# Gate/up products of two pairs of chunks in Strassen form (seven block products for eight), weight sums made by VectorE

## The reference, cut to what matters

```python
def swiglu(h, w_gate, w_up, w_down):
    return (jax.nn.silu(h @ w_gate) * (h @ w_up)) @ w_down
# four times:  x = x + 0.5 * swiglu(rms_norm(x, g), w_gate, w_up, w_down)
# once:        x = x + (silu(gate) * up) @ w_down,  gate, up = split(h @ w_gate_up, 2)
```

## Time and profile before

| | |
|---|---|
| time, median of 3 runs | 1306.96 us (1306.62 to 1307.1) |
| the profiled execution, its own time | 1307.18 us |
| its span, first to last instruction | 1305.4 us |
| PE busy | 1289.2 us (99%) |
| PEld busy | 1081.4 us (83%) |
| DVE busy | 846.8 us (65%) |
| ACT busy | 654.5 us (50%) |
| granted TensorE clock, mean | 0.998 |

### The profile page before, as it was taken

One profiled execution on the slowest core, in us unless ns is written; L12 is line 12 of the kernel. 1 busy time (PEld: TensorE's weight loads), 2 busy tenths in 40 slices (PEclk: granted clock), 3 DMA queues, 4 the chain that ended last, 5 costly groups with the idle time before them and its releaser, 6 DMA issues.

```text
span 1305.4 us, 17052 instructions
## 1 busy us (share of the span) xinstructions
PE 1289.2 (99%) x6249; PEld 1081.4 (83%) x6249; DVE 846.8 (65%) x929; ACT 654.5 (50%) x769; POOL 83.1 (6%) x195
## 2 busy tenths in 40 slices
PE   9999999999999999999999999999999999999997
PEld 7888889888888887888888877888888987888886
DVE  5665559876555567655556976555567887655554
ACT  6444457445444447544445865444447555544442
POOL 2000004100000002000001300000001300000000
PEclk9999999999999999999999999999999999999999
DMA  9776755446666745666663326666645551676771
GB/s 296 239 231 225 225 194 168 155 136 216 222 225 225 229 173 193 211 225 224 225 225 125 133 97 219 224 225 225 225 177 162 187 175 57 206 226 224 226 227 69
DMA packets 189563, 256.87 MB, mean 197 GB/s; under 512 B 9048, under 2 KB 151022, under 8 KB 189518
## 3 DMA queue, kind: packets, MB, share of 16 engines
q1 hardware_dynamic: 156560, 229.17, 53.3%
q10 hardware_dynamic: 32478, 26.30, 6.4%
q0 software_dynamic: 480, 0.80, 0.4%
HBM read 243.38 MB, written 12.85 MB: 196 GB/s over the span
## 4 chain that ended last, share of the span: by engine, by line
PE 96%; DVE 2%; ACT 1%; issue 0%; POOL 0%; POOLq 0%; DVEq 0%; ACTq 0%
PE ps L275 28%; PE ps L277 28%; PE ps L276 28%; PE ps L372 1%; PE ps L302 1%; PE ps L303 1%; PE ps L304 1%; DVE wl L247 1%; PE ps L1242 1%; PE ps L2972 0%; PE ps L666 0%; PE ps L281 0%; PE ps L2290 0%; PE ps L282 0%; PE ps L285 0%
## 5 line engine op out<-in xcount | busy, mean ns | idle before, releaser
L275 PE MATMUL ps<-wl,hth 128*128 128x512 f32 (+3 forms) x1256 | 490.1, 390 | 1.5 <-DVE htl L2148 0.8
L277 PE MATMUL ps<-wh,htl 128*128 128x512 f32 (+3 forms) x1256 | 485.0, 386 | 0.0
L276 PE MATMUL ps<-wh,hth 128*128 128x512 f32 (+3 forms) x1256 | 484.6, 386 | 0.0
L894 DVE TENSOR_TENSOR wl<-raw,wh 128x2048 fp32r<-128x2048 f32 x120 | 275.1, 2292 | 189.6 <-ACT wh L821 184.4
L821 ACT ACTIVATE wh<-raw 128x2048 fp32r<-128x2048 f32 x120 | 229.5, 1913 | 155.4 <-DMA bounce<-xn 114.8
L275 PEld LDWEIGHTS ps<-wl,hth 128*128 128x128 f32 x1256 | 236.1, 188 | 49.8 <-issue 2.7
L277 PEld LDWEIGHTS ps<-wh,htl 128*128 128x128 f32 x1256 | 236.0, 188 | 47.5
L276 PEld LDWEIGHTS ps<-wh,hth 128*128 128x128 f32 x1256 | 236.2, 188 | 44.8
L247 DVE TENSOR_TENSOR wl<-raw,wh 128x2048 fp32r<-128x2048 f32 (+3 forms) x94 | 207.5, 2216 | 63.1 <-ACT wh L236 62.3
L236 ACT ACTIVATE wh<-raw 128x2048 fp32r<-128x2048 f32 (+3 forms) x94 | 173.5, 1852 | 59.2 <-PE ps L277 43.9
L275 PE MATMUL ps<-wl,prod_h 128*128 128x512 f32 x400 | 156.3, 391 | 0.0
(11 more groups left out here) (423 smaller groups left out, 992.6 us busy)
## 6 DMA issues: line engine op xcount, KB each, us to landing
raw<-in_ffn_w_down SPq DMA_DIRECT2D x88, 512.0 KB, 4.0
raw<-in_ffn_w_gate SPq DMA_DIRECT2D x86, 512.0 KB, 4.1
raw<-in_ffn_w_up SPq DMA_DIRECT2D x86, 512.0 KB, 5.1
raw<-in_w_gate_up SPq DMA_DIRECT2D x44, 512.0 KB, 4.8
raw<-in_even_w_in SPq DMA_DIRECT2D x24, 512.0 KB, 4.5
bounce<-xn ACTq DMA_DIRECT2D x45, 256.0 KB, 3.1
xn<-bounce ACTq DMA_DIRECT2D x45, 256.0 KB, 5.1
raw<-in_w_down SPq DMA_DIRECT2D x22, 512.0 KB, 4.2
```

The source lines that it names most:

```text
L275: nc.tensor.matmul(o, xh, b, start=first, stop=False)
L276: nc.tensor.matmul(o, xh, a, start=False, stop=False)
L277: return nc.tensor.matmul(o, xl, a, start=False, stop=last)
L894: nc.vector.tensor_tensor(wl[:, r, :], raw[:, r, :], wh[:, r, :].bitcast(f32), ALU.subtract)\
```

## The change

Chunks 3 and 4, and chunks 7 and 8, are done as pairs. For a pair, the input (row tile by half of the 1024 inputs) is a 2x2 matrix of blocks A, and the weights (half of the inputs by chunk) a 2x2 matrix of blocks B. Before, that is eight block products of 12 matmuls. Now it is seven (`quarter`, 12 matmuls each), on sums of blocks of A and sums of blocks of B:

- Sums of A (`mix_rows`, `mix_low_parts`) are made once in each FFN, by DVE and ACT. As the two row tiles have different norms, A is first multiplied by them: two `row_diagonals` on DVE, two small matmuls on PE (`turn_first`), one wide multiply on DVE, and four subtractions or additions.
- Sums of B are made for each pair: `far_sum`, two `near_sums`, `last_sum`, each one op of 128x2048 on DVE. Three of these, and with the slots b11, b21, b22 and the fourth sum seven blocks in all, are split into high and low (four slots before). The chunk c+1 of the pair has its weights loaded into the arena by `load_far`; one of its halves is loaded a second time, as b22.
- Results are put together by two `evict` on ACT and five `combine` on DVE (128x512 each).
- The order of slots becomes, for a pair c, c+1: b11, b21, b22, d(c-1), sum, then a(c+2), b(c+2), d(c+1), d(c). The loops are written out.

The diff, cut to its core (`SPARE` and the tiles in the arena are moved too; `load_slot` is used in place of the loop's own loads; `through(kind, c)` splits every slot up to that one; `sum_high_of` and `sum_low_of` are one 128x2048 op each on ACT and on DVE; `combine` waits for its quarters):

```diff
+        SUM1, SUM2, SUM3, HIGH1, HIGH2, HIGH3 = (1536 + SLOT * i for i in range(6))
+        MIX = 1536 + 6 * SLOT
...
+        PAIRS = (3, 7)
+        ORDER = [("a", 0), ("b", 0), ("a", 1), ("b", 1), ("d", 0)]
+        waiting, c = [1], 2
+        while c < NCH - 1:
+            if c in PAIRS:
+                ORDER += [("b11", c), ("b21", c), ("b22", c), ("d", waiting.pop(0)), ("sum", c)]
+                waiting, c = [c + 1, c], c + 2
+            else:
+                ORDER += [("a", c), ("b", c)] + [("d", w) for w in waiting]
+                waiting, c = [c], c + 1
+        ORDER += [("a", c), ("b", c)] + [("d", w) for w in waiting] + [("d", c)]
+        assert len(ORDER) == FFN_SLOTS
+        PLACE = {what: i for i, what in enumerate(ORDER)}
+        TURN = [c for kind, c in ORDER if kind == "d"]
+        summed = [base[s] + PLACE["sum", g] for s, name in enumerate(PLAN) if name == "ffn" for g in PAIRS]
...
+            if n in summed:
+                act.wait_ge(last_sum_ready, summed.index(n) + 1)
+            else:
+                act.wait_ge(raw_loaded[n % RING], 32 * loads_through(n))
...
+            def load_far(sp, q, c):
+                if q > 0:
+                    sp.wait_ge(sums_used, 3 * q)
+                for half, at in ((0, SUM1), (1, SUM3)):
+                    v = arena[:, at:at + SLOT].rearrange("p (k n) -> p k n", k=4)
+                    for dst, src in gate_up(v, half, c * HC + HC):
+                        sp.dma_start(dst, src).then_inc(sum_loaded[half], 16)
...
+                for q, g in enumerate(PAIRS):
+                    if i == PAIR_LOADS[g]:
+                        sp.wait_ge(weights_used, n + 2)
+                        load_far(sp, len(PAIRS) * f + q, g)
+        PAIR_LOADS = {g: (7 if q == 0 else PLACE["d", PAIRS[0]]) for q, g in enumerate(PAIRS)}
...
+            def turn_first():
+                pe.wait_ge(prod_ready, f * NCH + 1)
+                turn_product(0)
+                pe.wait_ge(mix_diag, f + 1)
+                for tt in range(TT):
+                    m = nc.tensor.matmul(ps[:, 1, tt * P:(tt + 1) * P], ones[:, :], diag[:, tt, :], start=True, stop=True)
+                m.then_inc(mix_row, 1)
+            def quarter(b, rows_h, rows_l, w_h, w_l, first, last):
+                for kk in range(4):
+                    w = slice(kk * 512, (kk + 1) * 512)
+                    m = product(bank(b), rows_h(kk), rows_l(kk), w_h[:, w], w_l[:, w], first and kk == 0, last and kk == 3, not first)
+                return m
...
+            def pair(c):
+                q = len(PAIRS) * f + PAIRS.index(c)
+                near = [of_tile(v, 0, 0) for v in (hth, htl)], [of_tile(v, 0, 1) for v in (hth, htl)]
+                pe.wait_ge(mix_low, f + 1)
+                pe.wait_ge(sum_low, 3 * q + 1)
+                quarter(3, *of_mix(2), *of_sum(HIGH3, SUM3), True, True).then_inc(sums_used, 1)
+                pe.wait_ge(prod_ready, f * NCH + TURN.index(c - 1) + 1)
+                quarter(0, *near[0], *of_slot("b11", c), True, True).then_inc(weights_used, 1)
+                pe.wait_ge(sum_low, 3 * q + 2)
+                quarter(2, *of_mix(0), *of_sum(HIGH1, SUM1), True, True).then_inc(sums_used, 1)
+                pe.wait_ge(evicted, 2 * q + 1)
+                quarter(0, *near[1], *of_slot("b21", c), False, True).then_inc(weights_used, 1)
+                pe.wait_ge(sum_low, 3 * q + 3)
+                quarter(1, *of_mix(1), *of_sum(HIGH2, SUM2), True, True).then_inc(sums_used, 1)
+                pe.wait_ge(evicted, 2 * q + 2)
+                quarter(2, *of_mix(3), *of_slot("b22", c), False, True).then_inc(weights_used, 1)
+                down(c - 1)
+                pe.wait_ge(combined, 5 * q + 1)
+                quarter(3, *of_mix(4), *of_slot("sum", c), False, True).then_inc(weights_used, 1)
+                pe.wait_ge(combined, 5 * q + 4)
...
+            pe.wait_ge(mix_ready, f + 1)
+            waiting, c = [1], 2
+            while c < NCH - 1:
+                if c in PAIRS:
+                    pair(c)
+                    waiting, c = [c + 1, c], c + 2
+                else:
+                    plain(c)
+                    for w in waiting:
+                        down(w)
+                    pe.wait_ge(prod_ready, f * NCH + TURN.index(c) + 1)
+                    waiting, c = [c], c + 1
...
-            def split(c, j):
-                r = (n + j) % RING
-                act.wait_ge(raw_loaded[r], c * 32 + 32 * ((n + j) // RING + 1))
-                act.wait_ge(weights_used, c * 3 + (n + j - RING + 1))
-                nc.scalar.activation(wh[:, r, :], raw[:, r, :], ACT.Copy).then_inc(high_ready, 1)
...
+            def evict(c, j):
+                if j == 0:
+                    act.wait_ge(weights_used, n + PLACE["b11", c] + 1)
+                    nc.scalar.activation(near_1, bank(0), ACT.Copy, scale=rstd[:, 0:1]).then_inc(evicted, 1)
+                else:
+                    act.wait_ge(sums_used, 3 * pair_of(c) + 2)
+                    nc.scalar.activation(far_1, bank(2), ACT.Copy).then_inc(evicted, 1)
...
+            late, c = None, 2
+            while c < NCH - 1:
+                if c in PAIRS:
+                    evict(c, 0)
+                    high(c - 1)
+                    through("d", c - 1)
+                    evict(c, 1)
+                    through("sum", c)
+                    silu(c + 1)
+                    act_ahead.through(act, n + PLACE["sum", c] + 1)
+                    move_out(c + 1)
+                    silu(c, (0,))
+                    move_in(c + 1)
+                    act_ahead.through(act, n + PLACE["sum", c] + 2)
+                    silu(c, (1,))
+                    act_ahead.through(act, n + PLACE["sum", c] + 3)
+                    high(c + 1)
+                    move_out(c)
+                    act_ahead.through(act, n + PLACE["sum", c] + 4)
+                    move_in(c)
+                    late, c = c, c + 2
+                    continue
+                pair_next = c + 1 in PAIRS
+                if pair_next:
+                    sum_high_of(c + 1, 1, HIGH3, SUM3)
+                    through("b11", c + 1)
+                    sum_high_of(c + 1, 2, HIGH1, SUM1)
+                    sum_high_of(c + 1, 3, HIGH2, SUM2)
+                elif late is None:
+                    through("a", c + 1)
+                silu(c)
+                if late is not None:
+                    high(late)
+                    through("a", c + 1)
+                    late = None
+                through(*(("b21", c + 1) if pair_next else ("b", c + 1)))
                 move_out(c)
-            act_ahead.n += 3 * (NCH - 3)
-            move_in(NCH - 2)
-            act_ahead.through(act, n + FFN_SLOTS - 2)
-            high(NCH - 2)
-            act_ahead.through(act, n + FFN_SLOTS - 1)
-            silu(n + 3 * (NCH - 1) + 1)
+                if pair_next:
+                    through("b22", c + 1)
+                move_in(c)
+                if not pair_next:
+                    through("d", c)
+                    high(c)
+                c += 1
+            silu(c)
...
+            def mix_rows():
+                v = rows_turned
+                dve.wait_ge(mix_row, f + 1)
+                dve_link(dve, nc.vector.tensor_tensor(v, v, repeated(bank(1, T), 1, KT), ALU.mult))
+                a11, a12, a21, a22 = (v[:, 4 * half:4 * half + 4, tt * P:(tt + 1) * P] for tt in range(TT) for half in range(2))
+                nc.vector.tensor_tensor(mixed(2), a11, a21, ALU.subtract)
+                dve_link(dve, nc.vector.tensor_tensor(mixed(0), a21, a22, ALU.subtract))
+                dve_link(dve, nc.vector.tensor_tensor(mixed(1), mixed(0), a11, ALU.subtract))
+                nc.vector.tensor_tensor(mixed(3), mixed(1), a12, ALU.add).then_inc(mix_ready, 1)
...
+            def far_sum(c):
+                q = pair_of(c)
+                for loaded in sum_loaded:
+                    dve.wait_ge(loaded, 32 * (q + 1))
+                nc.vector.tensor_tensor(sum_of(SUM3), sum_of(SUM3), sum_of(SUM1), ALU.add).then_inc(sum_ready, 1)
+            def near_sums(c):
+                q = pair_of(c)
+                w = raw_of("b11", c)
+                dve.wait_ge(sum_ready, 3 * q + 1)
+                dve.wait_ge(mix_low, f + 1)
+                nc.vector.tensor_tensor(sum_of(SUM1), sum_of(SUM1), w, ALU.add).then_inc(sum_ready, 1)
+                nc.vector.tensor_tensor(sum_of(SUM2), sum_of(SUM3), w, ALU.add).then_inc(sum_ready, 1)
+            def last_sum(c):
+                p = n + PLACE["sum", c]
+                dve.wait_ge(split_ready, p - RING + 1)
+                dve.wait_ge(sum_ready, 3 * pair_of(c) + 3)
+                nc.vector.tensor_tensor(raw[:, p % RING, :], sum_of(SUM2), raw_of("b21", c), ALU.add).then_inc(last_sum_ready, 1)
...
+            row_diagonals()
...
+            turned_rows()
             low_turned(0, 0, prod_l, prod_h)
             dve_ahead.through(dve, n + 5)
-            multiply(1, 2)
```

(68 more changed lines are left out.)

308 lines of the change are left out of this document (206 added, 102 removed).

## The result

| | before | after |
|---|---|---|
| time, median (range) | 1306.82 us (1306.62 to 1307.1) | 1399.6 us (1395.32 to 1406.4) |
| ratio to before, 95% interval | 1 | 1.0715 [1.0671, 1.0758] |
| profiled execution: span | 1305.4 us | 1398.4 us |

The changed kernel is slower by 92.8 us, 7.1%. The direction was forecast, the size was not: 1399.6 lies above the range of 1313 to 1362.

The account below looks back on a forecast made before the run. PE, busy 99% of the span, was taken as the bound, with DVE's order deciding its stalls. -26.1 + 27.7 + 14 + 12.5 = +28.1 us on 1307.18 gave 1335.3; with 5 for the clock, 1340 us, range 1313 to 1362.

Parts of the forecast that it names:

- What PE gains: 120 matmuls fewer in five FFN save 27.2 us, ten matmuls with `ones` add 1.1: net 26.1 us.
- The first pair: Before each FFN's first pair, PE waits for `multiply(2)` behind DVE's queue: 4.2, three times 5.4 and 7.3, 27.7 us.
- The second pair: Before each FFN's second pair, PE waits for `multiply(6)`, behind chunk 5's bounce and DVE's sums: 2.8 us five times, 14 us.
- Inside and behind a pair: Small waits, mostly for the bounce of the pair's second chunk: 1.25 us a pair, 12.5 in all (0 to 25).
- this rival: The bounce collides with the far loads: 2.2 us more at ten pairs, 22 in all, 1357 to 1362; chance 0.1.
- The clock: Half clock behind PE's stalls costs at most 1.6 us a stall, 16 for ten; a third taken, 5 us.
- The forecast's own test: Wrong if wide sums cost less than a split, `multiply(2)` comes within 22 us of b(1), or a wait inside is longer.

Follow-up runs that it names:

- kernel 3: Changed kernel, with SyncE holding the loads behind slots d(3) and d(7), second pair's far weights included, until the bounce of chunk 3 (7) landed: 1383.3 us.
- kernel 11: Kernel 10 with each pair's first chunk bounced through DRAM again, not transposed by TensorE, and the second pair's far weights held until that bounce landed: 1336.9 us.
- kernel 2: Changed kernel, with idle transposes on TensorE at its long waits: 34 before the first pair, 34 and 24 before the down products of chunks 3 and 7: 1385.0 us.
- kernel 6: Kernel 4 with the last chunk's split of d(10) moved ahead (1336.7 us), plus 34 unread transposes on TensorE before its wait for the first pair: 1329.6 us.
- kernel 9: Kernel 4 with the split of d(10) moved ahead (1336.7 us), plus pairs one chunk later and the far sum moved earlier: 1345.5 us.
- kernel 10: Kernel 9 with only the order of each pair's preparation changed on VectorE and ScalarE, and TensorE beginning a pair with b11's product: 1306.3 us.
- kernel 4: Changed kernel, with the product of chunks 3 and 7 transposed by TensorE in place of the bounce through DRAM: 1343.8 us.

## Why the prediction was wrong

The frame held: the matmuls are saved, VectorE's order gives it all back and more, and the kernel is slower. Step by step:

- **What PE gains**, -26.1: measured -23.3 for the matmuls alone. Small. The products with `ones` came as 20 records, not 10, some 2 us in place of 1.1.
- **The first pair**, 27.7: measured 21.0, 4.2 in each FFN. The schedule by hand was right to 0.2 us in f = 1. In f = 0 part of the lack came earlier, as the wait of 2.33 us for `multiply(1)`, which the forecast does not have; with it the stall is 6.5 (7.3 forecast). In f = 2, 3 and 4 TensorE waited there too, for 0.14 to 0.20 us. From that release on, both engines have the same work ahead in these four FFN, which is why the stall is 4.2 in each (5.4 forecast for three).
- **The second pair**, 14: measured 5. The chain took 12.3 us where I had 12.0, but it began 5.0 us after the start of a(6) and not 7.1 (433.28 and 428.26). The step had the wrong wait: chunk 5's bounce had landed at 424.55, before a(6) began, and `high(5)` stood behind ScalarE's split of d(5), which TensorE releases at the start of a(6):

```profile
428.52 1.92 ACT L271 ACTIVATE wh<-raw 128x2048 fp32r<-128x2048 f32 x1 [4.59 <-PE ps L312]
430.35 0.61 ACT L959 ACTIVATE prod_h<-xn 128x512 fp32r<-128x512 f32 x1
```

- **Inside and behind a pair**, 12.5 (0 to 25; its own terms, 0.15, 0.1 and 42.0 - 41.1, make 1.15 a pair, not 1.25): measured 43.7. **This is the step that failed.** The place was right, and inside the pair there was no wait over 0.64 us. The bounce was priced at 8.4 us by the medians of the earlier trace rows; it took 13.1 to 15.7 at chunk 3 and 10.3 to 13.6 at chunk 7. Those rows are of a kernel in which one slot load at a time stood beside a bounce. In the new order SyncE sends a burst of slots just ahead, and at chunk 3 2 MB of far weights with it, and the engines are full (kernels 3 and 11). I named this rival, and gave it 2.2 us a pair more, from the slowest landings of before; the waits came to 3.1 a pair more than forecast, with half clock on top. The forecast had the waits before the pairs at over half of the idle time; they were 26 of 85.4 us, and those behind the pairs were half. A landing time under a load that the old trace never has can't be bounded by that trace's slowest.
- **The end of an FFN**: 7.6 us that the prediction does not have. I read the loops around a pair and not the lines behind them, where d(10) is no longer split ahead.
- **The clock**, 5 (up to 16): measured 28.9 us, 146 matmuls begun at half clock, 0.425 us apart on average in place of 0.227 (the expectation of kernel 2 has 0.416 and 27.6). This term was mis-sized next to the failed one. The price of a stretch was not far off: 15 stretches of 3.41 or 6.83 us lose TensorE 1.9 us each on average, where I had at most 2.7, or 1.6 net. (At the start of the program, from which I took it, the rows of the granted clock read 1.00, so that level was read from durations alone; the changed kernel's stretches bear the factor out.) But I took a third of the bound, for ten stalls. The stalls of 1.0 us before the second pairs brought none, those before the first pairs five, the waits behind the pairs nine and the end of an FFN one, and most of the loss came through in the time (kernels 2 and 6).

The sum by measured parts: -23.3 + (85.4 - 4.8) + 28.9 = 86.2 of 92.8 us. Most of the other 6.6 are some 2 us for the products with `ones` and a pitch of 0.2279 us where the kernel before has 0.2269, over some 4600 matmuls 4.6 us. Where the pitch comes from stays open.

The forecast's own test said that a wait for an `evict` or a chain of under 22 us would speak against me. Neither occurred; it did not test the landing times, on which the step hung.

## What to carry to other kernels

When a change puts work on an engine whose total has room, write down what stands in front of each operation that the critical engine waits for: here five wide operations in front of one multiply came with a kernel 39 us slower than the same work in another order (kernels 9 and 10), more than the 23 us of matmuls saved. A latency taken from a trace holds only for the load beside it; when the change moves DMAs, price the bounce with the queue full, or take it off the DMA engines (55.8 us, kernel 4). Saving 2% of the matmuls by a scheme with more small steps broke even at best here, with everything hidden.

## What the hardware showed beyond that

- An operation of VectorE with two operands in SBUF waits for a running operation of GpSimd to end (25 of 25 cases, up to 6.7 us for 2.29; 0.69 became 4.8 on average for `prod_l`), one with a PSUM operand does not. The Trainium skill (SBUF — State Buffer, Who interferes with whom) says that a VectorE instruction with two SBUF inputs contends with GpSimd's reads. The trace agrees, and shows that it waits in full.
- In the changed kernel half clock came in stretches of 3.41 or 6.83 us and was granted 2.7 to 5.7 us after the last matmul ahead of a stall began, so mostly behind it, on work. Each stall of 2.8 us or more brought one, those of 1.0 us none, and of the six from 1.26 to 2.33 us one did (2.11 us, at the end of an FFN).
- Thirty-four fp32 transposes in 3.87 us kept the full clock over a wait of 4.2 us (kernel 6: 3.4 us of half clock left of 34.1). The Trainium skill (TensorE: Matmul & The Clock Gate, Part 4) says that transposes do not count as work for the clock in the same way. By that the half clock behind the first pairs would have stayed; here, in fp32, the transposes held the full clock.
